# Twelve instead of four dots for the 32 sparse tokens in the middle of the fill of a two-layer encoder trunk

## The reference

```
def peer(xn, wq, subkeys, u, v):
    ...                                    # per token 8 heads x 16 experts of 128 x 128, with weights g
    def one_block(args):
        xb, eb, gb = args
        ub = u[eb]
        hid = jax.nn.gelu(jnp.einsum('td,thkd->thk', xb, ub), approximate=False)
        vb = v[eb]
        return jnp.einsum('thk,thkd->td', (gb * hid).astype(vb.dtype), vb)
    ...
```

## Time and profile before

| | |
|---|---|
| median of 3 runs | 2048.75 us (2047.99 to 2051.69) |
| the profiled execution | 2048.55 us |
| its span | 2046.8 us |
| TensorE busy | 2032.6 us, 99% |
| VectorE busy | 1628.2 us, 80% |
| ScalarE busy | 1242.8 us, 61% |
| GpSimd busy | 853.0 us, 42% |
| moved by DMA | 446.85 MB, mean 218 GB/s |

### The profile page before, as it was taken

One profiled execution on the slowest core, in us unless ns is written; L12 is line 12 of the kernel. 1 busy time (PEld: TensorE's weight loads), 2 busy tenths in 40 slices (PEclk: granted clock), 3 DMA queues, 4 the chain that ended last, 5 costly groups with the idle time before them and its releaser, 6 DMA issues.

```text
span 2046.8 us, 40235 instructions
## 1 busy us (share of the span) xinstructions
PE 2032.6 (99%) x14054; PEld 1877.7 (92%) x14054; DVE 1628.2 (80%) x2766; ACT 1242.8 (61%) x2055; POOL 853.0 (42%) x470
## 2 busy tenths in 40 slices
PE   9999999999999999999999999999999999999999
PEld 7877889999999999999988778899999999999998
DVE  5867877987888688888868678679788886888887
ACT  5855545467888555444568555554688885544444
POOL 2300005988887722122013000069888877221220
PEclk9999999999999999999999999999999999999999
DMA  7444564556555688999754445645565556998995
GB/s 250 150 153 146 182 195 155 195 195 209 194 186 180 213 315 311 308 311 316 243 199 156 149 147 183 203 153 195 195 207 196 180 186 224 316 315 302 313 313 193
DMA packets 122895, 446.85 MB, mean 218 GB/s; under 512 B 13968, under 2 KB 13968, under 8 KB 122256
## 3 DMA queue, kind: packets, MB, share of 16 engines
q1 hardware_dynamic: 102528, 371.24, 53.8%
q0 software_dynamic: 18432, 67.12, 10.1%
q10 hardware_dynamic: 1808, 6.89, 1.0%
HBM read 443.10 MB, written 1.05 MB: 217 GB/s over the span
## 4 chain that ended last, share of the span: by engine, by line
PE 93%; DVE 4%; ACT 2%; issue 1%; DMA 0%; DVEq 0%; ACTq 0%
PE ps L1008 21%; PE ps L610 17%; PE ps L611 17%; PE ps L612 17%; PE ps L1010 10%; PE ps L618 3%; PE ps L974 3%; PE ps L620 1%; PE ps L629 1%; DVE w_lo L1489 1%; PE ps L934 1%; PE ps L755 1%; ACT w_hi L1099 1%; PE ps L828 0%; PE ps L714 0%
## 5 line engine op out<-in xcount | busy, mean ns | idle before, releaser
L1008 PE MATMUL ps<-wgt,w_hi 128*128 128x448 f32 x2048 | 642.1, 374 | 0.0
L612 PE MATMUL ps<-hT,w_lo 128*128 128x224 f32 x2048 | 561.3, 274 | 0.0
L611 PE MATMUL ps<-hT,w_hi 128*128 128x224 f32 x2048 | 561.2, 274 | 0.0
L610 PE MATMUL ps<-hT,w_hi 128*128 128x224 f32 x2048 | 560.5, 274 | 0.0
L1010 PE MATMUL ps<-wgt,w_lo 128*128 128x224 f32 x2048 | 541.2, 264 | 0.0
L1308 ACT ACTIVATE w_hi<-raw 128x1024 fp32r<-128x1024 f32 x512 | 516.2, 1047 | 8.7 <-PE ps L612 5.8
L557 POOL TENSOR_TENSOR w_lo<-raw,w_hi 128x1024 fp32r<-128x1024 f32 x176 | 422.9, 2420 | 71.8 <-ACT w_hi L1308 70.6
L1008 PEld LDWEIGHTS ps<-wgt,w_hi 128*128 128x128 f32 x2048 | 384.1, 188 | 29.1
L612 PEld LDWEIGHTS ps<-hT,w_lo 128*128 128x128 f32 x2048 | 393.2, 192 | 0.0
L611 PEld LDWEIGHTS ps<-hT,w_hi 128*128 128x128 f32 x2048 | 392.8, 192 | 0.0
L610 PEld LDWEIGHTS ps<-hT,w_hi 128*128 128x128 f32 x2048 | 392.8, 192 | 0.0
(11 more groups left out here) (224 smaller groups left out, 2999.3 us busy)
## 6 DMA issues: line engine op xcount, KB each, us to landing
raw<-in_w_u SPq DMA_DIRECT2D x256, 512.0 KB
raw<-in_w_v SPq DMA_DIRECT2D x256, 512.0 KB
raw<-in_stream SPq DMA_DIRECT2D x192, 512.0 KB
arena<-in_bias ACTq DMA_DIRECT2D x2, 1024.0 KB, 5.5
arena<-in_subk ACTq DMA_DIRECT2D x2, 1024.0 KB, 4.9
x<-in_x SPq DMA_DIRECT2D x4, 256.0 KB, 4.8
arena<-x ACTq DMA_DIRECT2D x8, 128.0 KB, 3.0
arena<-in_gain_rows ACTq DMA_DIRECT2D x2, 512.0 KB, 6.0
```

The source lines that it names most:

```text
L610: mm(out_, left[0], right[0], start=start, stop=False, skip_group_check=group)
L611: mm(out_, left[0], right[1], start=False, stop=False, skip_group_check=group)
L612: return mm(out_, left[1], right[0], start=False, stop=stop, skip_group_check=group)
L1008: mm(ps[:, c, 0:2 * DENSE], w_hi[:, 2 * k + e, dims], wgt[:, k, e, :, :].rearrange("p a b -> p (a b)"), start=first, stop=False, skip_grou ...
```

## The change

`FILL_DOTS` has 15 entries instead of 7: the dots at pairs 39, 40 and 41 stay, and before them twelve stand at pairs 8, 10, 12, 15, 17, 19, 22, 24, 27, 29, 32 and 34 instead of four at 8, 14, 21 and 29. By that 17 instead of 25 dots stand beside the down products, at p = 3 to 19 instead of 3 to 27. `FIRST_SUM` gets 8 more, so that the share-out and the sums stay at p = 29 and on. GpSimd's gathers follow `STEPS`: twelve instead of four of them are issued in the fill behind the first three, at pairs 10 to 36, and the first three of the down table at p = 20, 21 and 22 instead of 28, 29 and 30.

```
-FILL_DOTS = (8, 14, 21, 29, FILL - 3, FILL - 2, FILL - 1)
+FILL_DOTS = (8, 10, 12, 15, 17, 19, 22, 24, 27, 29, 32, 34, FILL - 3, FILL - 2, FILL - 1)
 STEPS = list(FILL_DOTS)
 STEPS += [FILL + 3 + i for i in range(SPARSE - len(STEPS))]
-FIRST_SUM = STEPS[-1] + 2 - FILL
+FIRST_SUM = STEPS[-1] + 2 - FILL + 8
 STEPS += [FILL + FIRST_SUM + i for i in range(SPARSE)]
 LAST_SUM = STEPS[-1] - FILL
```

## The result

The changed kernel takes 2057.91 us (median of 6 runs, 2056.6 to 2059.86) against 2048.73 for the kernel before (6 runs beside it): ratio 1.0045, 95% interval 1.0034 to 1.0055. It is 9.2 us slower; 6.8 were forecast. The execution profiled took 2059.86 us, with a span of 2058.1.

The account below looks back on a forecast made before the run. TensorE, 93% of the chain, was taken as the bound. Per layer 3.0 + 0.6 + 1.0 - 1.2 = 3.4 us lost in the fill, 0 in the down products; both layers 6.8, giving 2055.6 us, range 2049.5 to 2068.

Parts of the forecast that it names:

- dots in single pairs: Fill, six dots at pairs with one router group: 0.5 us lost each, 3.0 per layer (bounds 1.8 to 11.4).
- the walk: Waits followed from pair 10's dot: nothing lost if it gets in between splits, 1.9 us after one more split.
- evenly spread: Fill: the point where a dot meets a split spread over 2.4 us; 58% lose 0.1 us, the rest 1.1.
- dots in doubled pairs: Fill, six dots at pairs with two router groups, idle time behind: 0.1 us each, 0.6 per layer (0 to 1.8).
- seven intervals of two pairs: Fill, dots only two pairs apart: lateness isn't made up, 0.15 us each, 1.0 per layer.
- the four dots of before: Fill of the kernel before: its four middle dots already lose about 0.3 us each, 1.2 per layer, subtracted from the sum.
- the gathers: Fill, GpSimd's queue: waiting 1.90 us for the dot and 0.96 for the issue stay covered by a margin, so 0.
- the backlog: GpSimd in the fill: its queued splits don't drain with dots two pairs apart, 11.8 of 12.14 us being taken.
- The dots hide: Rival, 28%: VectorE's idle time in the fill takes the dots; 0 to 1.2 us more, 2048.8 to 2050.
- VectorE becomes the bound: Rival, 15%: in the fill the dots exceed VectorE's idle time, 8 to 12 us per layer; 2073 us.
- The down products got no faster: Judges the 4% rival: pairs 20 to 27, without dot and gather, run under 4.8 us instead of 5.0; about 2041.
- 53 matmuls in the windows: Sign in the down products: TensorE starts 53 matmuls in 8 us everywhere, whatever VectorE, GpSimd and DMA do.

Follow-up runs that it names:

- e1: Changed kernel with its twelve middle dots all at pairs with two router groups (7, 9, 11 to 30): 2049.47 us, ratio 1.0008 to the kernel before.
- e2: Changed kernel with its twelve middle dots all at pairs with one router group (8, 10, 12 to 31): 2072.73 us, ratio 1.0116 to the kernel before.
- e3: Changed kernel with the twelve middle dots of the fill left out, all gathers kept: 2045.38 us, ratio 0.9985 to the kernel before.
- e6: Kernel before with its four middle dots at pairs with two router groups (7, 11, 20, 24): 2046.67 us, ratio 0.9992 to the kernel before.
- e7: Kernel before with its four middle dots left out, gathers kept: 2045.74 us, ratio 0.9988 to the kernel before.
- e4: Changed kernel with the twelve middle dots replaced by a sum with one SBUF input: 2045.29 us, ratio 0.9986 to the kernel before.
- e5: Changed kernel with the twelve gathers in the fill left out, the dots kept: 2056.34 us, ratio 1.0039 to the kernel before.

## Why the prediction was right, and where its sizes were off

**The bound.** Shown. TensorE's pace in the down products didn't move with VectorE, GpSimd or DMA (53 or 54 matmuls in each of the four windows; 321.4 us in before, after, e1, e2, e3, e6 and e7; e3 against e7), so the half of the change that takes dots away had nothing to win.

**The mechanism in the fill.** Shown. The dot waits for GpSimd's split (e4, and `make_hot`), and VectorE's lateness reaches TensorE through ScalarE's weighing of the one-hot rows (the waits at 528.32 and 532.38), above all where the dot has waited for a whole split and the next pair's group follows at once (e2). With lone dots of equal length it reaches TensorE at single pairs and not at doubled ones (before against e6). That a dot in a doubled pair would also hide a wait of a whole split isn't shown.

**The sum.** 6.8 forecast, 9.2 measured, 9.6 by the starts of the router groups. Per layer:
- dots in single pairs: 3.0 forecast, 4.8 measured. The two levels of the walk were right: nothing when the dot gets in at the end of a split, and for a whole split more 1.3 to 1.6 (1.9 in the walk). The share was not: I had the dots meet the splits evenly spread, with a mean of 0.5; the six lost 0.24, 1.49, 0, 1.26, 0.25 and 1.58, a mean of 0.8. The places aren't independent. A dot delays ScalarE, which delays the splits, and the next dot two pairs later meets them where the last one left them; e2 shows this, with nine of twelve dots at 3.42 to 3.48 us. And there is luck in the total: the dot of pair 12 came in by some tenths of a us, and where it didn't (e5, first layer), a layer lost 1.4 more.
- dots in doubled pairs: 0.6 forecast, 1.2 measured, growing through the fill from 0 (pairs 15, 17) to 0.39 (pair 34). That the products that weigh a pair grow by then, and leave less idle time, fits; it wasn't tested by itself.
- seven intervals of two pairs: 1.0 forecast. There is no such term of its own: e1 has ten of them and loses 1.85 in all. What I had put there belongs to the single pairs, as above. By that a part of the 1.8 that was missing in the first term was made up by a term that doesn't exist.
- the four dots of before: 1.2 forecast, 1.25 measured.
- the gathers: 0 forecast, 0 measured without dots (e3). With dots they shift which of them meets a whole split (e5), which the forecast left out.
- the backlog, on which the even spread rested. It is there behind the doubled pairs 15 and 17: from 555.7 to 568.1 GpSimd has a gather, four splits and 1.90 us of waiting for the next dot, and nothing between them. It isn't behind pairs 8 and 10, where 1.16 us of idle time stand ahead of three splits (515.78), nor in e2's settled state. Of the three costly dots only that of pair 19 came out of a backlog.

**The rivals.** "The dots hide" is true of the dots of pairs 12, 15 and 17 only, and nearly so of all twelve in e1. "VectorE becomes the bound" would have been right for e2: 2 x (13.56 - 1.25) = 24.6 us, as the 24 of that rival. It isn't a bound by its work, since the waits of the dots for a split make it. The dots of 6.35 us (pair 41 still has one) stayed out of the middle of the fill. The down products got no faster.

**Signs named beforehand.** Right: 53 matmuls in the windows, router groups waiting behind single pairs, a longer fill (4.8 us instead of 3.4). Dots lay between 1.44 and 3.75 us, with a mean of 2.88 instead of 2.5, and 27.0 us stay before L1989, not 20.

## What to carry to other kernels

Before work is moved to another stage, ask which operands it reads and what the neighbouring engine does there: the same VectorE instruction took 1.22 us beside the down products and 2.9 beside GpSimd's splits, and one with a single SBUF input took 1.21 beside the same splits. In a tight chain of engines a place can be worth more than a load, by what the instruction meets on the other engine and by what stands behind it: here twelve instructions put in front of an idle stretch cost 0.6 us per layer more than the four of before, the same twelve one pair to the side 12.3. And work taken from a stage whose bound engine keeps an even pace (the same count in every window, whatever the others do) gave nothing back here.

## What the runs showed of the hardware that I had not expected

- GpSimd's splits and VectorE's dots fall into step. With a dot every two pairs at single pairs, the splits come every 13.57 us and each dot waits for a whole one, although GpSimd has 1.2 us of idle time ahead of three splits and 1.9 ahead of the gather.
- The exclusion works both ways. A dot that gets in first makes the split behind it take 3.38 (pair 12 of the changed kernel) or 3.49 us (e5) instead of 2.40.
- A dot of 6.35 to 6.38 us stands at pair 41 in each of the nine kernels, whatever came before. Two splits in a row go ahead of it, although the first begins 0.5 us after it. In before and after TensorE has no wait there (690 to 725 us). Why it doesn't get in between the two, as that of pair 40 does, stays open.
